# Summing all picked expert rows on TensorE, and a new place for the mixer's last blocks

## The reference

```python
x = x + mixer(x, ...)
x = x + mem_cross_attn(x, mem, ...)
h = rmsnorm(x, g_peer)
q = (h @ w_pq).reshape(T, 8, 2, 128)
s = einsum('thpk,hpnk->thpn', q, sub_keys)        # 8 heads, 2 sides, 128 keys
sv, si = top_k(s, 16)                             # per side
cand = sv[:, :, 0, :, None] + sv[:, :, 1, None, :]
cv, ci = top_k(cand, 16)                          # 16 experts of a head, 128 of a token
gate = softmax(cv)
ub, vb = u_tab[idx], v_tab[idx]                   # 128 rows of each table for a token
act = gelu(einsum('td,tkd->tk', h, ub)) * gate
x = x + einsum('tk,tkd->td', act, vb)
y = rmsnorm(x, g_final)
```

## Time and profile before

| | us |
|---|---|
| median of 3 runs | 4206.65 (4201.58 to 4211.75) |
| the profiled execution | 4207.68 |
| its span, first to last instruction | 4205.9 |
| PE busy | 3529.9 (84%) |
| DVE busy | 2854.5 (68%) |
| POOL busy | 1683.5 (40%) |
| ACT busy | 1651.5 (39%) |

### The profile page before, as it was taken

The page is one execution under the profiler, slowest core; times in us unless marked ns, Lnnn a source line. Parts: engine busy times, 40 slices in busy tenths (PEclk is TensorE's granted clock), DMA queues, the critical chain, the costliest instruction groups (busy, mean ns, idle before and its releaser), DMA issues.

```text
span 4205.9 us, 38714 instructions
## 1 busy us (share of the span) xinstructions
PE 3529.9 (84%) x8236; PEld 1523.6 (36%) x8236; DVE 2854.5 (68%) x5860; ACT 1651.5 (39%) x4381; POOL 1683.5 (40%) x1485
## 2 busy tenths in 40 slices
PE   8999989877878888888888887887897888888677
PEld 4554444332333333333333333333333333333222
DVE  2346971368496886785795795796786787687654
ACT  4343232024344444344444444444344444344333
POOL 0001232034334444444444444444444444445465
PEclk9999999988999999999999999999999999999889
DMA  3002556189989999999999999999999999999998
GB/s 106 30 30 93 187 177 232 46 340 386 419 328 421 421 412 421 417 407 415 416 404 420 420 399 416 416 400 420 418 407 413 415 406 417 421 403 419 421 422 350
DMA packets 210702, 1462.98 MB, mean 348 GB/s; under 512 B 25616, under 2 KB 25744, under 8 KB 41872
## 3 DMA queue, kind: packets, MB, share of 16 engines
q0 software_dynamic: 194880, 1377.92, 80.2%
q1 hardware_dynamic: 15568, 82.43, 5.4%
HBM read 1424.61 MB, written 35.65 MB: 347 GB/s over the span
## 4 chain that ended last, share of the span: by engine, by line
DVE 30%; DMA 25%; PE 15%; issue 9%; POOL 5%; DVEq 4%; ACT 3%; ACTq 1%; POOLq 0%; PEldq 0%
DMA arena<-in_uv,arena 24%; DVE arena L998 10%; PE ps L1428 7%; POOL arena L541 5%; DVE arena L950 5%; PE ps L1465 3%; PE ps L1414 3%; DVE arena L1092 1%; DVE arena L1089 1%; DVE arena L1094 1%; DVE arena L1014 1%; DVE arena L1041 1%; DVE arena L1075 1%; DVE arena L1081 1%; DVE arena L1051 1%
## 5 line engine op out<-in xcount | busy, mean ns | idle before, releaser
L1428 PE MATMUL ps<-arena 128*128 128x512 f32 x4400 | 2154.3, 632 | 597.1 <-ACT arena L717 581.5
L541 POOL DMA_INDIRECT arena<-in_uv,arena x1280 | 1552.9, 1213 | 1712.3 <-PE ps L1428 925.1
L998 DVE SCALAR_TENSOR_TENSOR arena<-arena 128x1024 f32<-128x1024 f32 x1280 | 1548.0, 1223 | 801.4 <-DMA arena<-in_uv,arena 767.3
L1428 PEld LDWEIGHTS ps<-arena 128*128 128x128 f32 x4400 | 829.2, 198 | 1857.4 <-ACT arena L717 1020.2
L710 ACT ACTIVATE acts<-dots 128x1 f32<-128x1 f32 x1280 | 258.6, 202 | 1794.8 <-DVE arena L998 1770.7
L1465 PE MATMUL ps<-arena 128*128 128x512 f32 x1280 | 585.1, 601 | 0.0
L717 ACT ACTIVATE arena<-ident,gated 128x128 f32<-128x128 f32 x1100 | 441.7, 402 | 80.4 <-issue 5.9
L1465 PEld LDWEIGHTS ps<-arena 128*128 128x128 f32 x1280 | 249.1, 195 | 314.3 <-issue 314.3
L1312 PE MATMUL ps<-arena 128*128 128x512 f32 (+1 forms) x768 | 279.2, 523 | 3.5 <-DVE arena L838 2.9
L1014 DVE SCALAR_TENSOR_TENSOR arena<-arena,gated 128x1024 f32<-128x1024 f32 x170 | 217.6, 1280 | 0.8 <-ACT gated L712 0.8
L712 ACT ACTIVATE gated<-arena,acts 128x1 f32<-128x1 f32 (+1 forms) x640 | 188.5, 294 | 62.0
(11 more groups left out here) (187 smaller groups left out, 2102.2 us busy)
## 6 DMA issues: line engine op xcount, KB each, us to landing
arena<-in_items SPq DMA_DIRECT2D x32, 1024.0 KB, 5.4
arena<-in_uv,arena POOLq DMA_INDIRECT x1280
qk_scratch<-arena POOLq DMA_DIRECT2D x32, 256.0 KB, 2.8
wp_scratch<-arena POOLq DMA_DIRECT2D x32, 256.0 KB, 6.0
vo_scratch<-arena POOLq DMA_DIRECT2D x32, 256.0 KB, 2.6
arena<-qk_scratch SPq DMA_DIRECT2D x2, 4096.0 KB, 14.4
arena<-vo_scratch SPq DMA_DIRECT2D x2, 4096.0 KB, 21.9
arena<-wp_scratch SPq DMA_DIRECT2D x2, 4096.0 KB, 27.1
```

The lines of the kernel that those rows point to most:

```text
L541: g.indirect_dma_start(out=ring[r], out_offset=None, in_=a["uv"], in_offset=bass.IndirectOffsetOnAxis(ap=IDXC[:, k:k + 1], axis=0))\
L998: v.scalar_tensor_tensor(out=ring[r][:, 0:D], in0=ring[r][:, 0:D], scalar=1.0, in1=H[par], op0=ALU.mult, op1=ALU.mult, accum_out=dots[:, r ...
L1428: ins = t.matmul(ACC[par][:, half * BANK:(half + 1) * BANK], diag[r], ring[r][:, D + half * BANK:D + (half + 1) * BANK], start=False, stop ...
```

## The change

All 128 picks of a block go the way over TensorE. The functions that chose the engine, VectorE's sums, the accumulator, the merge and their four semaphores are gone. A gather waits for `row_used` alone, and so does `final_squares`; the last pick of a block ends the sum in PSUM (`stop=last`). Apart from this, the first quarter's six top-k pieces get the turns 72, 72, 75, 75, 78 and 78, so that VectorE takes block 7 between the second and the third piece, block 8 between the fourth and the fifth, and block 9 behind the sixth.

```diff
-DVE_FIRST, DVE_END = 2, 8
-def by_dve(group):
-    return (1, 3, 5) if DVE_FIRST <= group < DVE_END else ()
...
-             q=((66, 66), (1, 1), (9, 12), (21, 24)), choose=[[72] * 6] + steps(-8, 2)[1:])
+             q=((66, 66), (1, 1), (9, 12), (21, 24)), choose=[[72, 72, 75, 75, 78, 78]] + steps(-8, 2)[1:])
...
-        ACCV = piece(D)
...
             def gather(b, k):
                 r = k % R
-                if k >= R and on_dve(k - R):
-                    hold(row_summed, b * DVE_PICKS + dve_rank(k - R) + 1)
-                else:
-                    hold(row_used, b * PE_PICKS + (k + 1 if k < R else R + pe_rank(k - R) + 1))
+                hold(row_used, b * PICKS + k + 1)
...
-                ins = act.activation(gated[:, r:r + 1], GAT[par][:, ds(k, 1)], ACT.Copy, scale=acts[:, r:r + 1])
-                if summed_by_dve:
-                    ins.then_inc(gated_ready, 1)
-                    return
+                act.activation(gated[:, r:r + 1], GAT[par][:, ds(k, 1)], ACT.Copy, scale=acts[:, r:r + 1])
                 act.drain()
...
             def final_squares(b, par):
-                act.wait_ge(merged, b + 1)
+                act.wait_ge(row_used, R + (b + 1) * PICKS)
...
-            def pick(b, par, group, r, slots):
+            def pick(b, par, group, r):
                 v.wait_ge(row_load[r], (b * GROUPS + group) * 16 + 16)
                 v.scalar_tensor_tensor(out=ring[r][:, 0:D], ..., accum_out=dots[:, r:r + 1]).then_inc(dot_ready, 1)
-                s = r - LAG
-                if s not in slots:
-                    return
-                ...
-                hold(gated_ready, ...)
-                    ins = v.scalar_tensor_tensor(ACCV, rows, gated[:, s:s + 1], ACCV, ALU.mult, ALU.add)
-                ins.then_inc(row_summed, 1)
...
-            def pick(n, par, r):
+            def pick(n, par, r, last=False):
                 t.wait_ge(diag_ready, n + 1)
                 for half in range(2):
                     ins = t.matmul(ACC[par][...], diag[r],
-                                   ring[r][...], start=False, stop=False)
+                                   ring[r][...], start=False, stop=last)
                 ins.then_inc(row_used, 1)
...
-            def merge(b, par):
-                t.wait_ge(row_summed, (b + 1) * DVE_PICKS)
-                for half in range(2):
-                    ins = t.matmul(ACC[par][...], ident[:, :], ACCV[...], start=False, stop=True)
-                ins.then_inc(merged, 1)
```

More of the change, by code:

```diff
@@ L93 @@
 GROUPS = PICKS // R
-LAG = 2
 assert GROUPS * R == PICKS
-DVE_FIRST, DVE_END = 2, 8
-def by_dve(group):
-    return (1, 3, 5) if DVE_FIRST <= group < DVE_END else ()
[L105 to L119, removed]
-def stretch(at, end):
[L124 to L129, removed]
+def stretch(at, end):
+    return (end - at) // R if at % R == 0 else 0
 def steps(first, every):
@@ L705, in hold, with pick @@
                 act.sem_inc(act_held, 1)
-            def pick(b, par, k, r, summed_by_dve):
+            def pick(b, par, k, r):
                 act.wait_ge(dot_ready, b * PICKS + k + 1)
@@ L726, in walk @@
                             for r in range(R):
-                                pick(b, par, i * R + (at + r), r, on_dve(at + r))
+                                pick(b, par, i * R + (at + r), r)
                         at += whole * R
                     else:
-                        pick(b, par, at, at % R, on_dve(at))
+                        pick(b, par, at, at % R)
                         at += 1
             def final_squares(b, par):
-                act.wait_ge(merged, b + 1)
+                act.wait_ge(row_used, R + (b + 1) * PICKS)
                 act.activation(PF[1], ACC[par], ACT.Square, accum_out=fms)
@@ L1000, in pick @@
                  .then_inc(dot_ready, 1)
-                s = r - LAG
-                if s not in slots:
-                    return
[L1004 to L1013, removed]
-                    ins = v.scalar_tensor_tensor(ACCV, rows, gated[:, s:s + 1], ACCV, ALU.mult, ALU.add)
-                ins.then_inc(row_summed, 1)
             def walk(b, par, at, end):
                 while at < end:
-                    whole = stretch(at, end) if at // R != DVE_FIRST else 0
+                    whole = stretch(at, end)
                     if whole:
@@ L1023, in walk @@
                             for r in range(R):
-                                pick(b, par, i + at // R, r, by_dve(at // R))
+                                pick(b, par, i + at // R, r)
                         at += whole * R
                     else:
-                        pick(b, par, at // R, at % R, by_dve(at // R))
+                        pick(b, par, at // R, at % R)
                         at += 1
@@ L1428, in pick @@
                     ins = t.matmul(ACC[par][:, half * BANK:(half + 1) * BANK], diag[r],
-                                   ring[r][:, D + half * BANK:D + (half + 1) * BANK], start=False, stop=False)
+                                   ring[r][:, D + half * BANK:D + (half + 1) * BANK], start=False, stop=last)
                 ins.then_inc(row_used, 1)
@@ L1434, in walk @@
                 while at < end:
-                    whole = stretch(at, end)
-                    if whole:
+                    whole = stretch(at, min(end, PICKS - R))
+                    if whole > 0:
                         with t.Fori(0, whole) as i:
                             for r in range(R):
-                                if not on_dve(at + r):
-                                    pick(b * PE_PICKS + i * (R - len(by_dve(at // R))) + pe_rank(at + r), par, r)
+                                pick(b * PICKS + i * R + (at + r), par, r)
                         at += whole * R
                     else:
-                        if not on_dve(at):
-                            pick(b * PE_PICKS + pe_rank(at), par, at % R)
+                        pick(b * PICKS + at, par, at % R, at == PICKS - 1)
                         at += 1
-            def merge(b, par):
-                t.wait_ge(row_summed, (b + 1) * DVE_PICKS)
-                for half in range(2):
-                    ins = t.matmul(ACC[par][:, half * BANK:(half + 1) * BANK], ident[:, :],
-                                   ACCV[:, half * BANK:(half + 1) * BANK], start=False, stop=True)
-                ins.then_inc(merged, 1)
             def transposes(dst, src):
```

5 lines of the change are left out of this document (removed).

## The result

The median of the changed kernel is **4181.89 us** (4180.46 to 4184.63, five runs), that of the kernel before, run beside it, 4203.57 (4200.94 to 4211.75). The ratio is 0.9946, with an interval from 0.9931 to 0.996: 21.7 us less. The forecast was 4185, within 4174 to 4203. The profiled execution took 4180.93 us, 26.8 less than the profiled one of before; some 5 us of that are scatter between executions, as the medians show.

What follows compares the result with a forecast made beforehand. Transfers bound most stretches, VectorE the top-k picks 69 to 117. 4207.7 - 13.7 (seam) - 8 (block 0) - 1.7 (merge) + 2 (TensorE's load) = 4186.3, the median 1.0 lower: 4185 us, range 4174 to 4203.

Steps and rivals of the forecast that it cites:

- The seam: At 800 to 862 us, before the first gather: new top-k order removes TensorE's 12.00 us wait, 13.7 us earlier.
- The reload of x: Before mixer block 9: x tile reload asked for at about 818, some 17 us before it is needed.
- the rival in which the seam fails: Before the first gather: a reload wait or top-k behind the fetches takes back 13.7 us, 4199 us; chance 8%.
- Block 0: Picks 4 to 38 of block 0: without VectorE's sums 8 us off, bounds 4 and 9.7.
- The merge: Between the last pick and the final squares: four matmuls fewer, 1.7 us off the last path.
- TensorE's added load: Picks 17 to 64: 18 more rows, 30.9 us a block, just fit; 2 us lost in all, bounds 0 and 20.
- VectorE's margin at pick 69: First top-k piece of a middle block: product ends 2.1 us before VectorE asks; added lag of 1.4 leaves 0.7.
- The room of 4.0 us a block: Picks 17 to 64 of a middle block: TensorE needs 115.0 us of 119.0 after the change.
- the rival of a recovering top-k stretch: Picks 69 to 117: fuller ring regains half the lost rate, 2.8 us in eight blocks, 4162 us; chance 6%.
- mostly sooner: Gathers that waited for VectorE's sum, some 5 us after the row's dot, now wait for TensorE, mostly less long.
- What a lag would cost: At pick 69, once the margin is gone, each further us costs one us in each of eight blocks.
- Weight loads in line: Picks 17 to 64: 260 loads add 51 us, 47 over the transfers in each of eight blocks, about 4560; chance 1%.

Runs made afterwards that it cites:

- the sums alone: The changed kernel with the first quarter's six top-k pieces back at turn 72: 4194.42 us, ratio 0.9973 to the kernel before.
- the seam alone: The kernel before with only the new turns of the first quarter's six top-k pieces, VectorE still summing 18 rows a block: 4195.03 us, ratio 0.997.
- records added: Sixteen more matmul records on TensorE in blocks 1 to 8: in one piece, changed kernel 4222.57 us, kernel before 4222.96; in eight parts, 4210.6 and 4206.62.
- the top-k spread: The changed kernel with the 24 top-k pieces of blocks 1 to 8 at every 2.4 picks instead of every 2: 4182.25 us, ratio 0.994.
- the spread records: Sixteen more matmul records in blocks 1 to 8, two ahead of each half product: changed kernel 4210.6 us, ratio 1.0007; kernel before 4206.62 us, ratio 1.0.
- block 1's steps later: The changed kernel with block 1's attention three picks and its top-k one pick later inside block 0: 4188.57 us, ratio 0.9957.
- one sum of three left on VectorE: The kernel before with the new seam turns and 6 rows a block summed by VectorE instead of 18: 4184.74 us, ratio 0.9951.

## Why the prediction was right

The total fell where it was forecast because two terms were off in opposite directions: block 0 gave less, and blocks 1 to 8 gave some 5 us where a loss of 2 was forecast. That these nearly cancel is luck. Step by step:

- **The seam: right.** 13.7 forecast, 13.2 measured; the waits of 0.6 and 1.1 us that the layout had for TensorE are there as 0.57 and 0.99. The reload of x is no limit, and the rival in which the seam fails is out.
- **Block 0: direction right, size wrong.** 8 us forecast, bounds 4 to 9.7. Measured are 2.2 in the pair of profiles and 5.7 with the sums alone; four profiles with VectorE's sums in block 0 show 382.6 to 385.6 us (before, the seam alone, both with records added in blocks 1 to 8), five without them 376.9 to 380.8 (changed, the sums alone, two with records added, the top-k spread), 4.5 us between the means. So it is about half of the forecast. The step up to pick 38 was right: it comes 106.2 us after the first dot instead of 114.7, 8.4 less, and the rates follow (first and second line below, against 341 and 348 in the earlier trace rows). The step that failed is that the gain was taken to stay. Here are the stretches behind, and ScalarE's and TensorE's waits, in the changed kernel:

```profile
935.70:952.80 17.10, 14.54 (x34) 5.84 (x33) 16.39 (x60) 5.97 (x20) 9.01 (x8) 1.00 1.01 422
952.80:972.90 20.10, 13.73 (x31) 5.10 (x29) 16.30 (x35) 9.54 (x25) 9.70 (x9) 1.00 1.02 420
972.90:999.00 26.10, 21.37 (x51) 9.88 (x52) 13.26 (x22) 14.79 (x42) 9.30 (x8) 0.87 0.94 374
999.00:1020.00 21.00, 21.00 (x50) 9.31 (x49) 10.60 (x17) 7.21 (x25) 8.73 (x9) 1.00 1.01 414
1020.00:1036.50 16.50, 16.50 (x46) 7.75 (x45) 8.01 (x14) 8.88 (x25) 9.34 (x8) 1.00 0.98 365
...
972.44 1.03 ACT L658 ACTIVATE ps<-arena 128x1024 f32<-128x1024 f32 x1 [3.58 <-DMA arena<-x_scratch]
...
977.63 7.41 PE L1375 MATMUL ps<-arena 128*128 128x512 f32 x12 [5.59 <-ACT arena L679]
```

Picks that come earlier reach the first step that needs block 1's x before it is loaded: ScalarE waits 3.58 us, its next diagonals come late, TensorE idles 5.59 us and then runs without a gap while the rate dips to 374 and 365. At pick 69 only 2.3 us of the 8.4 are left. And the block's end hangs on a product and 112 us of VectorE behind it, not on pick 38. I had looked at the stretch in which the sums lie, and not at what ends the block. Why the product came at 268.4 us here and at 264.7 with the sums alone, where ScalarE waited 3.08 us for x as well, is not settled; 2.6 of these 3.7 us are there at pick 69 already (185.6 against 183.0).
- **The merge: right.** 1.7 forecast, 1.7 measured.
- **TensorE's added load: mechanism right, sign of the term wrong.** Its part up to pick 69 came as forecast: 1.1 us more in the eight blocks (0 to 2), TensorE 99% busy at a clock of 1.00 and 419 GB/s. Inside it the time moves: picks 16 to 38 take 5.7 us less and picks 38 to 69 take 7.4 more, and so it is, within 1 us, with the sums alone and with the top-k spread. VectorE's margin at pick 69 is 0.9 to 2.0 us over the eight blocks (0.7 forecast), and it never waits there. The room of 4.0 us a block was 2 to 3.7 by the spread records. But I had excluded a gain, by the rate in picks 17 to 64 alone. Picks 69 to 117 take 5.1 us less in eight blocks (989.2 against 984.1). VectorE has a wait there that the rows on record don't show: in every block of the kernel before, the dot of pick 72 or 74 waits for its transfer. Here is that of block 4, and below it the gather of block 4's pick 69, in the kernel before and in the changed one:

```profile
2421.63 1.23 DVE L998 SCALAR_TENSOR_TENSOR arena<-arena 128x1024 f32<-128x1024 f32 x1 [0.94 <-DMA arena<-in_uv,arena]
...
2396.84 1.02 POOL L541 DMA_INDIRECT arena<-in_uv,arena  x1 [2.68 <-issue]
...
2374.91 1.35 POOL L506 DMA_INDIRECT arena<-in_uv,arena  x1 [1.12 <-issue]
```

These waits come to 6.8 us in the eight blocks, to 6.0 with the seam alone and 6.9 with the spread records in the kernel before. In the changed kernel five of the eight are gone and 2.4 us are left, with the sums alone 2.4, with block 1's steps later 3.2. So some 4 of the 5 us are transfers that are further ahead of VectorE when the top-k pieces begin. That is what the rival of a recovering top-k stretch named, and "VectorE itself has no gap there", which spoke against it, was not quite so. But its 22 us took the missing rate for time that could be had. Only the 6.8 us of waits could; the rest is VectorE's own work, as the forecast said. The gathers point to what made the difference. Pick 69 lies in slot 5, after pick 61. Where VectorE sums pick 61, the gather of pick 69 is issued 13.1 to 13.4 us ahead of its dot (in block 4, 2396.84 for a dot at 2409.99); in the changed kernel it is 15.2 to 16.3 (2374.91 for 2390.89), with the sums alone 15.3 to 16.3. With one sum of three left on VectorE, in slot 3, it is 14.7 to 15.6 for pick 69, and for pick 67, in slot 3, the 18.1 to 18.4 before dot 69 that the kernel before has; VectorE's waits in picks 69 to 117 are gone there. I had written that TensorE gives such slots back "mostly sooner", and put it at nothing.
- **What a lag would cost: size about right, place wrong.** I wrote that past the margin each further us costs one in each block, as VectorE would wait for the product. The spread records go beyond the forecast room by 6.87 - 4.0 = 2.9 us a block, and cost 3.2. But it is in picks 27 to 69 that the time is lost, with TensorE busy without a gap (124.00 of 124.70 us in block 4); VectorE's waits for the first product come to at most 2.0 us in the eight blocks.
- **Weight loads in line: wrong by far, as forecast.** Of 120.20 us TensorE is busy 118.92 with 53.81 us of loads inside. The sentence in the section The mechanism of "TensorE: Matmul & The Clock Gate" in the Trainium skill, by which a load overlaps only where row groups differ, disagrees with this row; the section's other case, by which a load into the background weight buffer is pulled ahead of running matmuls as well, would fit, but no run here shows that it is the one.

## What to carry to other kernels

Work moved between engines in a stretch that waits for transfers is worth nothing there (picks 0 to 69: 1397.0 us before, 1398.1 after), though it can show in the next stretch; look for the few places outside it, here the seam, where one engine's order of work made another wait, and lay the new order out on a timeline before it is tried. For a gain in the middle of a stage ask what ends the stage: in block 0 it was a product and 112 us of packed work behind it, and of 8.4 us won at pick 38 about half was left at its end. Whether an engine has room is read from its waits, not from its busy share: VectorE, busy 94% in picks 69 to 117 of block 4, waited for nothing there after the change. When a full engine's room is tested with added work, spread that work; one burst measures the depth of the buffers instead.

## What the runs showed of the hardware

- In the kernel before, 10.3 us in which TensorE gives back none of the eight ring slots cost one pick, 2.45 us, in each block, though it has 16 us to spare in the stretch; 6.87 us of added work in eight parts cost nothing there (ratio 1.0).
- TensorE at 99% busy (300 records in 120.20 us, granted clock 1.00) and gathers at 419 GB/s go together; in the kernel before, with 226 records, the granted clock of the stretch was 0.91, so part of its busy 97.53 us was the low level.
- VectorE can be the limit at 94% busy: in picks 69 to 117 of block 4 in the changed kernel it is busy 115.51 of 122.60 us and waits for nothing; the rest is some 90 short gaps between its own instructions, 6.8 us in all.
- With the top-k pieces further apart, the transfers of picks 69 to 117 stay below the last block's pace (121.9 us for 48 picks, not 119) though VectorE waits for them 7.4 us in each block. No run here explains it.
